# The first MLP matrix by seven products of block sums instead of eight, in a two-layer trunk on one core

## The reference

```
h += s5_mixer(rmsnorm(h))                      # layer 0
h += attention(rmsnorm(h), k, v)               # layer 1, k and v shared
h += square(relu(rmsnorm(h) @ w_in)) @ w_out   # both layers, w_in 1024 x 4096, w_out 4096 x 1024
out = rmsnorm(h)
```

## Time and profile before

| what | value |
|---|---|
| median of 3 runs | 1050.72 us (1050.56 to 1051.0) |
| span of the profiled execution | 1048.7 us |
| TensorE busy | 1026.1 us, 98% of the span |
| VectorE busy | 557.4 us, 53% |
| ScalarE busy | 229.5 us, 22% |
| GpSimd busy | 693.3 us, 66% |
| mean granted TensorE clock | 0.993 of full |

### The profile page before, as it was taken

One profiled execution on the slowest core, in us unless ns is written; L12 is line 12 of the kernel. 1 busy time (PEld: TensorE's weight loads), 2 busy tenths in 40 slices (PEclk: granted clock), 3 DMA queues, 4 the chain that ended last, 5 costly groups with the idle time before them and its releaser, 6 DMA issues.

```text
span 1048.7 us, 15508 instructions
## 1 busy us (share of the span) xinstructions
PE 1026.1 (98%) x5626; PEld 834.1 (80%) x5626; DVE 557.4 (53%) x645; ACT 229.5 (22%) x512; POOL 693.3 (66%) x568
## 2 busy tenths in 40 slices
PE   9889999999999999999999999999999999999996
PEld 4677888888888888888887666888888888888886
DVE  7993446677317514713854675668751472273125
ACT  7863111211001000101312877221100010010011
POOL 8996866687667666766646330778776676677650
PEclk9899999999999999999999999999999999999999
DMA  6123322232222332233323110233222332223312
GB/s 249 38 44 125 110 103 94 80 121 95 92 94 101 100 100 89 93 100 101 100 81 101 41 59 3 81 117 101 94 93 97 101 100 101 85 95 100 101 61 81
DMA packets 35903, 97.49 MB, mean 93 GB/s; under 512 B 11144, under 2 KB 13704, under 8 KB 35600
## 3 DMA queue, kind: packets, MB, share of 16 engines
q1 hardware_dynamic: 35856, 96.83, 28.0%
HBM read 92.36 MB, written 2.10 MB: 90 GB/s over the span
## 4 chain that ended last, share of the span: by engine, by line
PE 87%; ACT 4%; DVE 4%; issue 2%; SPq 1%; DMA 1%; DVEq 0%; POOL 0%; POOLq 0%
PE ps L1268 24%; PE ps L1270 24%; PE ps L1269 24%; PE ps L1214 2%; PE ps L1216 2%; PE ps L1215 2%; SPq L314 1%; PE ps L1424 1%; PE ps L1399 1%; PE ps L1411 1%; DMA toep<-k_even 1%; ACT s_sb L647 1%; PE ps L1331 1%; PE ps L1330 1%; PE ps L1329 1%
## 5 line engine op out<-in xcount | busy, mean ns | idle before, releaser
L438 POOL TENSOR_TENSOR w_lo<-raw,w_hi 128x1024 fp32r<-128x1024 f32 x164 | 414.4, 2527 | 13.7
L1268 PE MATMUL ps<-hid,w_hi 128*128 128x512 f32 x704 | 275.9, 392 | 0.0
L1269 PE MATMUL ps<-hid,w_hi 128*128 128x512 f32 x704 | 274.2, 389 | 0.0
L1270 PE MATMUL ps<-hid,w_lo 128*128 128x512 f32 x704 | 274.2, 389 | 0.0
L350 POOL TENSOR_TENSOR gate_sb<-gate_sb 128x1 f32<-128x1 f32 x164 | 40.7, 248 | 307.6 <-PE ps L1270 268.4
L1268 PE MATMUL ps<-act,w_hi 128*128 128x512 f32 x464 | 180.7, 389 | 0.0
L1270 PE MATMUL ps<-act,w_lo 128*128 128x512 f32 x464 | 180.6, 389 | 0.0
L1269 PE MATMUL ps<-act,w_hi 128*128 128x512 f32 x464 | 180.6, 389 | 0.0
L435 POOL TENSOR_SCALAR w_hi<-raw 128x1024 fp32r<-128x1024 f32 x164 | 172.1, 1050 | 0.0
L1268 PEld LDWEIGHTS ps<-hid,w_hi 128*128 128x128 f32 x704 | 132.2, 188 | 27.8 <-issue 0.7
L1270 PEld LDWEIGHTS ps<-hid,w_lo 128*128 128x128 f32 x704 | 132.2, 188 | 27.8
(11 more groups left out here) (218 smaller groups left out, 1054.1 us busy)
## 6 DMA issues: line engine op xcount, KB each, us to landing
raw<-panels_in SPq DMA_DIRECT2D x164, 512.0 KB, 3.2
xy<-xu_in SPq DMA_DIRECT2D x4, 512.0 KB, 7.7
out<-h SPq DMA_DIRECT2D x8, 256.0 KB, 2.5
prm<-prm_in SPq DMA_DIRECT2D x1, 1280.0 KB, 6.0
h<-x_rows_in SPq DMA_DIRECT2D x1, 1280.0 KB, 12.8
h<-x_rows_in SPq DMA_DIRECT2D x1, 768.0 KB, 7.4
dd<-dd_in SPq DMA_DIRECT2D x1, 256.0 KB, 5.9
toep<-k_even SPq DMA_DIRECT2D x4, 64.0 KB, 2.4
```

The source lines that it names most:

```text
L438: nc.gpsimd.tensor_tensor(w_lo[:, s, :], raw[:, s % 2, :], w_hi[:, s, :].bitcast(F32), ALU.subtract).then_inc(w_split, 1)
L1268: mm(ps[:, bank, :], w_hi[:, s, w], x[:, 0, k, :], start=(k == 0), stop=False)
L1269: mm(ps[:, bank, :], w_hi[:, s, w], x[:, 1, k, :], start=False, stop=False)
L1270: last = mm(ps[:, bank, :], w_lo[:, s, w], x[:, 0, k, :], start=False, stop=(k == KT - 1))
```

## The change

In each MLP the first four panels of `w_in` stay units. The other 28 are taken as 14 pairs. A pair is a 2 x 2 grid of blocks (panel by half of the k tiles, 512 columns of `w_raw` each), the activations are a 2 x 2 grid too (half of the k tiles by half of the tokens). The four block products of each of the two panels, eight in all, become seven (`product`: A11, A12, S1, S2, S3, S4, A22). A product is 4 k tiles x 3 matmuls of 256 columns, into half a bank (banks 4 to 7). Four of its weight blocks are sums or differences of blocks, formed by VectorE (`sums_near`, `sum_all`); four of the activation operands, T1 to T4, are formed once per layer for four k (`t_blocks`, `t_his`) and lie in `hid[:, 1]`. Signs are carried along, so that one of two hidden tiles comes out negated (its relu is a minimum).

The split of the seven blocks moves from GpSimd to ScalarE (`s_round`, high parts) and VectorE (`rest`, low parts). SyncE loads a pair as one transfer of 1 MB (`load_pair`) once all splits of the pair before are done (`s_split`), in the same queue as the panels. The results are put together by ScalarE (two copies) and VectorE (five `join`s of 256 columns); the hidden tile's square moves from VectorE to ScalarE.

Between the products of a pair lie four half panels of `w_out` (`out_tile`, 12 matmuls of 512 columns, over four hidden tiles), each with its own addition to `h` (`add_out`): 48 such additions per layer and 8 whole units at the end, in place of 32 units. The last two pairs of a layer have no half panels beside them. TensorE waits for all T blocks (`t_lo`) before `stats`, and for rstd (`stat_a`) before the first product.

```
+A11, A12, S1, S2, S3, S4, A22 = range(7)
+RAW_OF = {A11: 1, A12: 2, S1: 3, S2: 5, S3: 0, S4: 5, A22: 4}
+SUM_OF = {S1: 1, S3: 1, S2: 2, S4: 3}
+T1, T2, T3, T4 = range(4)
...
+        w_raw = sb("w_raw", [P, 6, HK * P], where=over)
+        s_hi = sb("s_hi", [P, 7, HK * P], F32R, where=over)
+        s_lo = sb("s_lo", [P, 7, HK * P], F32R, where=over)
...
+        x1, y_, z_, w_ = (ps[:, b, 0:HALF] for b in (4, 5, 6, 7))
+        u2, u2z = acc[:, 0:HALF], acc[:, HALF:]
+        t_raws = {T1: y_, T2: w_, T3: z_, T4: ps[:, 7, HALF:]}
+        b12 = t_raws[T4]
+        sum_m, sum_n = t2[:, 0, :], t2[:, 1, :]
...
+            def load(first, end):
+                for u in range(first, end):
+                    wait(sp, w_split, u - 1)
+                    sp.dma_start(raw[:, u % 2, :], panels[u]).then_inc(raw_in[u % 2], 16)
+            def load_pair(n):
+                wait(sp, s_split, 7 * n)
+                sp.dma_start(w_raw[:, 1:5, :].rearrange("p b n -> p (b n)"), pairs[n]).then_inc(pair_in, 16)
+            def load_mlp(layer):
+                base, n0 = U_MLP[layer], PAIRS * layer
+                load(base, base + 1)
+                load_pair(n0)
+                load(base + 1, base + 7)
+                load_pair(n0 + 1)
+                load(base + 7, base + 9)
+                for n in range(2, PAIRS):
+                    load(base + 2 * n + 5, base + 2 * n + 7)
+                    load_pair(n0 + n)
+                load(base + 2 * PAIRS + 5, base + MLP_UNITS)
...
+            wait(sp, ot_lo, QUADS * NBLK)
+            load_mlp(1)
...
+            def t_his(layer, k, g):
+                n = 4 * (HK * layer + k)
+                scale = COLS(g)[:, k:k + 1]
+                wait(a, t_lo, n)
+                act_fn(b12, h[:, k, right], ACT.Copy, scale=scale).then_inc(b12_done, 1)
+                for i, t, factor in ((1, T1, 1.0), (3, T3, 1.0), (4, T2, -1.0), (4, T4, -1.0)):
+                    a.wait_ge(t_raw, n + i)
+                    act_fn(t_block(t, 0, k), t_raws[t], ACT.Copy, scale=factor).then_inc(t_hi, 1)
+            def s_round(n, blocks, freed):
+                a.wait_ge(pair_in, 16 * n + 16)
+                if freed is not None:
+                    a.wait_ge(prod_done, freed)
+                first, last = blocks[0], blocks[-1]
+                if first in SUM_OF:
+                    a.wait_ge(s_sum, 3 * n + SUM_OF[first])
+                act_fn(s_hi[:, first:last + 1, :].rearrange("p b n -> p (b n)"),
+                       w_raw[:, RAW_OF[first]:RAW_OF[last] + 1, :].rearrange("p b n -> p (b n)"),
+                       ACT.Copy).then_inc(s_hi_done, 1)
...
+                for blocks in ((A11, A12), (S1,), (S2,), (S3,), (S4,), (A22,)):
+                    s_round(n0, blocks, None if layer == 0 else 7 * n0)
...
+                def square(p, tile, i, at):
+                    a.wait_ge(relu_done, 2 * p + i + 1)
+                    act_fn(tile, tile, ACT.Square).then_inc(squared, 1)
+                    a.wait_ge(squared, 2 * p + i + 1)
+                    act_fn(hid[:, 0, 0, at, :], tile, ACT.Copy).then_inc(hid_hi, 1)
+                def step(p, q, following=True):
+                    at = HK * ((q // 2 + 1) % 2) + 2 * (q % 2)
+                    a.wait_ge(prod_done, 7 * p + A11 + 1)
+                    a.wait_ge(hid_lo, FB * HK * layer + HK + 2 * (p - n0) - 1)
+                    act_fn(sum_m[:, left], x1, ACT.Copy).then_inc(u1_done, 1)
+                    if following:
+                        s_round(p + 1, (A11, A12), 7 * p + A12 + 1)
+                        s_round(p + 1, (S1,), 7 * p + S1 + 1)
+                    a.wait_ge(prod_done, 7 * p + S2 + 1)
+                    a.wait_ge(joined, 5 * p + 5)
+                    act_fn(u2, x1, ACT.Copy).then_inc(u2_done, 1)
+                    if following:
+                        s_round(p + 1, (S2,), 7 * p + S2 + 1)
+                        s_round(p + 1, (S3,), 7 * p + S3 + 1)
+                        s_round(p + 1, (S4,), 7 * p + S4 + 1)
+                    square(p, sum_m, 0, at)
+                    if following:
+                        s_round(p + 1, (A22,), 7 * p + A22 + 1)
+                    square(p, sum_n, 1, at + 1)
...
+            def t_blocks(layer, k, g):
+                n = 4 * (HK * layer + k)
+                near, far = COLS(g)[:, k:k + 1], COLS(g)[:, k + HK:k + HK + 1]
+                v.wait_ge(b12_done, HK * layer + k + 1)
+                stt(t_raws[T1], h[:, k, left], near, b12, ALU.mult, ALU.subtract).then_inc(t_raw, 1)
+                stt(t_raws[T3], h[:, k + HK, right], far, b12, ALU.mult, ALU.subtract).then_inc(t_raw, 1)
+                v.wait_ge(t_raw, n + 2)
+                stt(t_raws[T2], h[:, k, left], near, t_raws[T3], ALU.mult, ALU.add).then_inc(t_raw, 1)
+                v.wait_ge(t_raw, n + 3)
+                stt(t_raws[T4], h[:, k + HK, left], far, t_raws[T2], ALU.mult, ALU.subtract).then_inc(t_raw, 1)
+                v.wait_ge(t_raw, n + 4)
+                for i, t, factor in ((1, T1, 1.0), (2, T3, 1.0), (4, T2, -1.0), (4, T4, -1.0)):
+                    v.wait_ge(t_hi, n + i)
+                    stt(t_block(t, 1, k), t_raws[t], factor, t_block(t, 0, k).bitcast(F32), ALU.mult, ALU.subtract
+                        ).then_inc(t_lo, 1)
...
+                def sums_near(n):
+                    v.wait_ge(pair_in, 16 * n + 16)
+                    tt(w_raw[:, 0:4:3, :], w_raw[:, 1:5:3, :], w_raw[:, 3, :].unsqueeze(1).to_broadcast([P, 2, HK * P]), add
+                       ).then_inc(s_sum, 1)
+                    v.wait_ge(s_sum, 3 * n + 1)
+                    tt(raw_block(S2), raw_block(S1), raw_block(A11), add).then_inc(s_sum, 1)
+                def sum_all(n):
+                    v.wait_ge(s_sum, 3 * n + 2)
+                    tt(raw_block(S4), raw_block(S2), raw_block(A12), add).then_inc(s_sum, 1)
+                def rest(n, blocks):
+                    first, last = blocks[0], blocks[-1]
+                    v.wait_ge(s_hi_done, 6 * n + (1 if first == A11 else first))
+                    if first in SUM_OF:
+                        v.wait_ge(s_sum, 3 * n + SUM_OF[first])
+                    tt(s_lo[:, first:last + 1, :].rearrange("p b n -> p (b n)"),
+                       w_raw[:, RAW_OF[first]:RAW_OF[last] + 1, :].rearrange("p b n -> p (b n)"),
+                       s_hi[:, first:last + 1, :].rearrange("p b n -> p (b n)").bitcast(F32), sub
+                       ).then_inc(s_split, len(blocks))
+                sums_near(p0)
...
+                rest(p0, (A22,))
...
+                def relu(p, i, tile, op):
+                    v.wait_ge(joined, 5 + 5 * p + 4 + i)
+                    stt(tile, tile, 0.0, rstd[:], op, ALU.mult).then_inc(relu_done, 1)
+                def low(p, i, tile, at):
+                    v.wait_ge(hid_hi, FB * HK * layer + HK + 2 * (p - p0) + i + 1)
+                    tt(hid[:, 0, 1, at, :], tile, hid[:, 0, 0, at, :].bitcast(F32), ALU.subtract).then_inc(hid_lo, 1)
+                def add_out(pp, q, j):
+                    m, a0 = HK * (q % 2) + j, n0 + 4 * pp + j
+                    if j % 2 == 0:
+                        v.wait_ge(half_done, 2 * N_OUT * 2 * layer + 2 * pp + j // 2 + 1)
+                    else:
+                        v.wait_ge(unit_done, base + MLP_OUT + 2 * pp + j // 2 + 1)
+                    v.wait_ge(h_added, a0)
+                    tt(h[:, m, :], ps[:, (j + shift) % 4, :], h[:, m, :], ALU.add).then_inc(bank_free, 1)
+                    v.wait_ge(bank_free, 4 + vb + HK + 4 * pp + j + 1)
+                    v.sem_inc(h_added, 1)
+                def join_11(p):
+                    v.wait_ge(u1_done, p + 1)
+                    v.wait_ge(prod_done, 7 * p + A12 + 1)
+                    tt(sum_m[:, left], sum_m[:, left], y_, add).then_inc(joined, 1)
+                def join_u4(p):
+                    v.wait_ge(u2_done, p + 1)
+                    tt(u2z, u2, z_, add).then_inc(joined, 1)
+                def join_22(p):
+                    v.wait_ge(prod_done, 7 * p + S3 + 1)
+                    v.wait_ge(joined, 5 + 5 * p + 2)
+                    tt(sum_n[:, right], u2z, w_, add).then_inc(joined, 1)
+                def join_12(p):
+                    v.wait_ge(prod_done, 7 * p + S4 + 1)
+                    tt(sum_m[:, right], u2, z_, add).then_inc(joined, 1)
+                def join_21(p):
+                    v.wait_ge(prod_done, 7 * p + A22 + 1)
+                    tt(sum_n[:, left], u2, w_, add).then_inc(joined, 1)
+                def step(pp, q):
+                    p = p0 + pp
+                    at = HK * ((q // 2 + 1) % 2) + 2 * (q % 2)
+                    join_11(p)
+                    sums_near(p + 1)
+                    rest(p + 1, (A11, A12))
+                    rest(p + 1, (S1,))
+                    add_out(pp, q, 0)
+                    join_u4(p)
+                    rest(p + 1, (S2,))
+                    sum_all(p + 1)
+                    add_out(pp, q, 1)
```

(125 more changed lines are left out.)

203 lines of the change are left out of this document (108 added, 95 removed).

## The result

The changed kernel takes 1147.01 us (median of 4 runs, 1145.77 to 1150.34) against 1050.86 us for the kernel before (4 runs, 1050.56 to 1051.54): ratio 1.0913, 95% interval 1.0893 to 1.0933. It is 96 us slower, where the prediction had 92 and gave slower 0.93. The profiled execution took 1150.34 us, 3 us more than the median; its span is 1148.5 us, 99.8 above that of before.

The account below looks back on a forecast made before the run. VectorE's loop, with contention from GpSimd, sets the pace: 1048.7 - 22.4 (TensorE) + 66 (waits in steps) + 44.3 (starts and ends) + 4 (clock) = 1140.6 us of span, plus 2 around it: 1142.6; range 1080 to 1190.

Parts of the forecast that it names:

- TensorE saves 22.4 us: Products of the 28 pairs: 10.1 us of TensorE per pair in place of 10.9, 0.8 us saved each.
- The loop of 23.7 us: Regular step: VectorE's list, the pair's landing and contention with GpSimd exceed TensorE's 20.96 us; TensorE waits 66 us in all.
- landing: Regular step: loading the next 1 MB pair takes 5.3 us, issue included, while VectorE's next sums wait for it.
- locks: Regular step: GpSimd's two w_out splits shut out VectorE operations with both inputs in SBUF, adding 4.6 us net.
- the rest of the list: Regular step: VectorE's work from landing to the end of A22 without contention, 13.8 us.
- `t_lo`: T blocks before the statistics: VectorE finishes them late, losing 0.5 us in layer 0 and 7 us in layer 1.
- rstd: MLP start: the first pair's split stands ahead of `inverse`, so the first product waits; 7.5 us lost per layer.
- The first step: Half panel 0 waits for four hidden tiles: 6.7 us idle, replacing the usual 2.7 and slack; nothing added.
- The last two pairs: Layer end without half panels: 31.1 us against 20.2 us of products, 10.9 us lost per layer.
- The clock, 4 us: Gaps of 7 us at the starts lower TensorE's clock: 1 us for each of four; gaps of some 2 us cost nothing.
- Rival 1: Regular steps: VectorE keeps up and TensorE sets the pace, leaving 34 us at starts and ends; 1062 us, chance 0.10.
- Rival 2: Whole kernel: VectorE's results are always ready and TensorE never waits, so it is faster; 1028 us, chance 0.05.
- Rival 3: TensorE's clock falls after each of 28 gaps, losing 1.5 us each time; up to 42 us, some 1180, chance 0.10.

Follow-up runs that it names:

- experiment 10: The kernel before, with the matmuls of 28 w_in panels per MLP each run as two of 256 columns: 1068.86 us, ratio 1.0166.
- experiments 1 to 4: Changed kernel, GpSimd's half-panel low part cut to 32 columns: 1081.95 us; formed twice: 1231.63; pair loaded in two transfers: 1111.9; each pair fetched twice: 1258.86.
- Experiment 5: Changed kernel with idle matmuls before the first product and in each step's gap before S1, to keep the clock up: 1130.9 us, ratio 1.0764.
- experiment 7: Changed kernel with the pair in two transfers and GpSimd's half-panel low part cut to 32 of 1024 columns: 1075.62 us, ratio 1.0235.

## Why the prediction was right

- **TensorE saves 22.4 us.** Right to 2 us. Products run at 0.120 us per matmul where unbroken, and experiment 10 measures the share that narrow matmuls take back. A half panel between products takes 2.74 us and not 2.72 (its first two matmuls are 0.23 and 0.24 apart), so TensorE's own step is 21.04 us and not 20.96.
- **The loop of 23.7 us.** Right as a whole (23.69), and in its mechanism (experiments 1 to 4). Its terms: landing 4.8, not 5.3; locks 4.3, not 5.3 (the 4.6 of the prediction is 5.3 less the 0.75 of waiting for ScalarE that passes under a lock); the rest of the list 14.1, not 13.8 less that 0.75, so 13.05; and 0.5 of waits for TensorE that I had not in it. Errors of up to 1 us in the terms cancelled: that the sum met the step to 0.01 us is luck. TensorE's idle in front of S1 was called 2.7 us in each of 24 steps: it is 2.4 in every second one, followed by a wait of about 1 us for a hidden tile and, mostly, by some microseconds at the lower clock. The total per step, which is what counts, is the same.
- **`t_lo`.** Layer 0 was to lose 0.5 us there and lost none. The statistics start at 189.69, before at 189.19 (the row at 189.62 is the second of their two matmuls), but TensorE doesn't wait in front of them, and it is already 0.5 us behind at 96 us, out of the mixer stage. In layer 1 they start at 753.81, before at 698.44; counted from the end of the MLP of layer 0 that is 8.6 us more than before, where 7 were predicted.
- **rstd.** First product forecast at 208.5 in layer 0, measured 209.84, idle 8.2 us for 7.5; in layer 1 4.8, so 13.0 for 15 in both.
- **The first step, "I add nothing".** This is the term that was mis-sized. The idle before half panel 0 is 6.0 us as computed (6.7), but it isn't hidden under VectorE's loop: VectorE waits for half panel 0, for the joins and for S3 and S4 in turn, 5.5 us in all, from 228.10 on. The step takes 28.2 and 26.9 us, 4.5 and 3.2 over a regular one. Experiment 5, with the clock held higher (0.83 at 220 to 230), still has 26.9 and 27.0, so most of it is that lateness and about 1.3 us of layer 0 the clock.
- **The last two pairs.** Final units start 19.0 us after the last landing; by the prediction's working that was 24.5 less the transfer's 5.3, 19.2. Right.
- **The clock, 4 us.** It fell where I expected (0.53 at 204 to 212) and also where the earlier trace rows had made me think that it wouldn't, after gaps of 2.4 us. In layer 0 it made VectorE wait 2.2 us for TensorE in two of ten steps, which then took 24.7 and 25.0 us. The price there is small because VectorE sets the pace; that it also moves the locks is left open (experiment 5).
- **The rivals.** Rival 1 (TensorE sets the pace, 1062) is what experiment 7 forces; it gives 1076, since I had the starts and ends at 34 us and they are 44, besides a step of 21.04 for 20.96. So even the favourable case was never faster. Rival 2 needed under 0.8 us of idle per pair, and the starts alone exceed that. Rival 3 gets the sign of the clock right and its size wrong.

Summed in the profiled execution: 99.8 us for 91.9 predicted. Counted from its statistics on, the MLP of layer 0 is 46.3 longer (42.2 predicted), that of layer 1 44.4 (42.2), the stretch between 8.6 (7.0), and what lies ahead 0.5 (0.5, but for another reason).

## What to carry to other kernels

An identity that saves multiplications in a kernel that TensorE bounds has to be paid in elementwise work: here 22 us less of TensorE in the whole program came with 269 us more of busy VectorE (557.4 to 826.2, locks included). So before counting products, walk the busiest other engine through one step, with the landing of its next data if the buffer is single, and compare that loop with TensorE's. VectorE operations with both inputs in SBUF and GpSimd's splits count as one queue: price a low part at what it takes beside the other engine's split, not alone. And every place where the new scheme starts or ends costs a full latency of the chain; 28 pairs in two stretches carried 44 us of such costs even in experiment 7, twice what the identity saved here.
